# Experts' weights in pairs of chunks: 2 MB transfers with 16 KB runs, eleven slots of two chunks, and the embeddings' product kept in DRAM until the last stage

## The reference

```python
proj = x @ w_in + b_in                       # 1024 -> 5192 columns
y_attn = sparse_attention(q, k, v, indexer, rel_bias) @ w_o_attn
y_conv = silu(layer_norm(causal_conv31(a * sigmoid(g)))) @ w_o_conv
mix = (sigmoid(g_attn) * y_attn + sigmoid(g_conv) * y_conv) @ w_out
x = layer_norm(alpha * x + mix)
# mixture of experts: 32 experts, 4 for each token
for e in range(32):
    g, u = split(x @ w_gate_up[e] + b_gate_up[e])        # 1024 -> 2 x 1024
    g, u = minimum(g, 7), clip(u, -7, 7)
    y = ((u + 1) * (g * sigmoid(1.702 * g))) @ w_down[e] + b_down[e]
    out += combine[:, e:e + 1] * y                        # zero for tokens not routed to e
h = alpha * x + out
x = layer_norm(h + sigmoid(h @ w_ple_gate) * (p @ w_ple_proj))
```

## Time and profile before

| | |
|---|---|
| median of 3 runs | 1247.0 us (1243.6 to 1247.7) |
| the profiled execution's own time | 1243.07 us |
| its span in the profile | 1241.3 us |
| PE busy | 1177.9 us, 95% |
| DVE, ACT, POOL busy | 292.2, 170.7, 7.1 us |
| moved by transfers | 446.12 MB, mean 359 GB/s |
| experts' weights | 384 transfers of 1 MB |
| granted PE clock, mean | 0.984 |

### The profile page before, as it was taken

How to read it: one execution, slowest core, us unless ns; L and a number is a source line. 1 busy time by engine, 2 the same in 40 slices (tenths; PEclk the granted TensorE clock), 3 DMA queues, 4 the chain that set the end, 5 groups by cost and what they waited for, 6 DMA issues and landing times.

```text
span 1241.3 us, 14072 instructions
## 1 busy us (share of the span) xinstructions
PE 1177.9 (95%) x5694; PEld 589.4 (47%) x5694; DVE 292.2 (24%) x753; ACT 170.7 (14%) x329; POOL 7.1 (1%) x28
## 2 busy tenths in 40 slices
PE   7999999989999999998989799999999999898987
PEld 6887888853443434343334333434344333333336
DVE  0506944331121111121110211111112111111125
ACT  1213122021111101110100111111111111011012
POOL 1000000000000000000000000000000000000000
PEclk9899999999999999999989899999999999999999
DMA  9961446549999999999999999999999999999990
GB/s 314 349 195 68 146 160 261 216 171 418 421 420 422 422 421 421 420 421 422 421 421 418 414 354 398 421 421 422 421 421 419 422 422 421 421 421 421 422 354 35
DMA packets 93419, 446.12 MB, mean 359 GB/s; under 512 B 10072, under 2 KB 40064, under 8 KB 44192
## 3 DMA queue, kind: packets, MB, share of 16 engines
q1 hardware_dynamic: 89776, 440.72, 88.0%
q10 hardware_dynamic: 3200, 3.18, 0.8%
q0 software_dynamic: 368, 1.19, 0.3%
HBM read 444.00 MB, written 1.06 MB: 359 GB/s over the span
## 4 chain that ended last, share of the span: by engine, by line
PE 60%; DMA 13%; DVE 3%; ACT 1%; issue 1%; SPq 0%; DVEq 0%; ACTq 0%
PE bank L342 47%; DMA ring<-in_w_gu 9%; PE bank L330 5%; DMA arena<-in_w_gu 4%; PE bank L363 3%; PE bank L1309 2%; PE bank L349 2%; PE bank L336 1%; ACT arena L1362 1%; DVE arena L389 1%; DVE arena L383 1%; DVE arena L407 0%; DVE arena L403 0%; PE bank L1240 0%; DVE arena L399 0%
## 5 line engine op out<-in xcount | busy, mean ns | idle before, releaser
L342 PE MATMUL bank<-ring,arena 128*64 128x512 f32 x2024 | 460.4, 607 | 26.2 <-DMA ring<-in_w_gu 13.6
L342 PEld LDWEIGHTS bank<-ring,arena 128*64 128x64 f32 x2024 | 144.8, 139 | 315.4 <-issue 289.7
L342 PE MATMUL bank<-arena 128*64 128x512 f32 x1144 | 256.3, 597 | 10.3 <-DMA arena<-in_w_gu 6.8
L383 DVE TENSOR_TENSOR arena<-bank,arena 128x512 f32<-128x512 f32 x33 | 22.8, 692 | 639.2 <-PE bank L349 639.2
L342 PEld LDWEIGHTS bank<-arena 128*64 128x64 f32 x1144 | 80.5, 137 | 169.2 <-issue 158.2
L569 PE MATMUL bank<-arena,ring 128*128 128x256 f32 x576 | 130.9, 389 | 7.3 <-DMA ring<-in_w_in 7.3
L569 PEld LDWEIGHTS bank<-arena,ring 128*128 128x128 f32 x576 | 112.0, 196 | 23.9 <-issue 8.3
L1362 ACT ACTIVATE arena<-bank 128x512 f32<-128x512 f32 x62 | 37.0, 598 | 428.1 <-PE bank L342 428.1
L363 PE MATMUL bank<-arena 64*128 64x512 f32 x272 | 67.6, 615 | 1.4 <-ACT arena L1365 1.4
L330 PEld LDWEIGHTS bank<-arena 128*128 128x128 f32 x512 | 58.4, 192 | 11.4 <-issue 11.4
L330 PE MATMUL bank<-arena 128*128 128x128 f32 x512 | 61.4, 278 | 0.0
(11 more groups left out here) (196 smaller groups left out, 541.7 us busy)
## 6 DMA issues: line engine op xcount, KB each, us to landing
ring<-in_w_gu SPq DMA_DIRECT2D x160, 1024.0 KB, 26.1
arena<-in_w_gu SPq DMA_DIRECT2D x96, 1024.0 KB, 26.3
ring<-in_w_dn SPq DMA_DIRECT2D x84, 1024.0 KB, 26.3
arena<-in_w_dn SPq DMA_DIRECT2D x44, 1024.0 KB, 26.1
ring<-in_w_in SPq DMA_DIRECT2D x19, 1024.0 KB, 12.0
ring<-in_w_out SPq DMA_DIRECT2D x4, 1024.0 KB, 5.1
ring<-in_w_pg SPq DMA_DIRECT2D x4, 1024.0 KB, 19.6
ring<-in_w_oa SPq DMA_DIRECT2D x2, 1024.0 KB, 5.0
```

What stands on the lines that cost most here:

```text
L342: mm = pe.matmul(to[half * CAP:(half + 1) * CAP, :], rows, w[:, half * 512:(half + 1) * 512], start=first, stop=last)
L383: nc.vector.tensor_tensor(by_bias(gt, 8), by_bias(of_gate[:, :], 8), bias_of(e, 0, 0, 8), ALU.add).then_inc(sw_step, 1)
```

## The change

The unit of the experts' weights becomes a pair of chunks: 2 MB, 6 of them to an expert (`CPE = 6`), with 16 KB in a row in each partition: two rows of gate-and-up or four of down. There are 11 slots of a pair (22 MB where 19 MB were): 6 are the ring, 5 in the arena. A slot is freed when PE has used both halves. To match the order of rows, `gather` reads every second column of x1, `turn` every fourth column of its input, and so do the last stage's transposes of h. `w_ple_gate` is loaded as two pairs of the same form. Room is made by storing `pple` in a DRAM buffer at the end of the front stage and loading it again at the end; SP waits for that store before it issues the load of pair 10, whose slot held `pple`. The order of the first 11 loads is new; the table's transfers move from POOL to ACT, and those of b_down's rows from POOL to SP. Products and sums are the same, apart from the order of the terms.

```diff
-ES = 19
+ES = 11
 SLOT = 2048
+PAIR = 2 * SLOT
...
-CPE = 12
-DOWN_ORDER = (0, 2, 1, 3)
+CPE = 6
...
         def slot_of(n):
             i = n % ES
-            return ring[:, (NF + i) % NS, :] if i < NS else extra[i - NS]
-        def chunk_source(e, c):
-            if c < KD:
-                return w_gu[bass.ds(e, 1), c * P:(c + 1) * P, :].rearrange("e p d -> p (e d)")
-            b = DOWN_ORDER[c - KD]
-            return w_dn[bass.ds(e, 1), b * 256:(b + 1) * 256, :].rearrange("e (p r) d -> p (e r d)", r=2)
...
+            if i >= NS // 2:
+                return extra[i - NS // 2]
+            i = 2 * ((NF // 2 + i) % (NS // 2))
+            return ring[:, i:i + 2, :].rearrange("p a d -> p (a d)")
+
+        def pair_source(e, c):
+            if c < 4:
+                return w_gu[bass.ds(e, 1), c * 256:(c + 1) * 256, :].rearrange("e (p r) d -> p (e r d)", r=2)
+            return w_dn[bass.ds(e, 1), (c - 4) * 512:(c - 3) * 512, :].rearrange("e (p r) d -> p (e r d)", r=4)
...
+        x1_rows = x1.rearrange("p t (c m r) -> p t c r m", c=4, r=2)
+        h_rows = h.rearrange("p t (c m r) -> p t c r m", c=2, r=4)
...
-                    mm = pe.matmul(bank[4 + k // 4][:, (k % 4) * P:(k % 4 + 1) * P], x1[:, t, k * P:(k + 1) * P],
+                    mm = pe.matmul(bank[4 + k // 4][:, (k % 4) * P:(k % 4 + 1) * P], x1_rows[:, t, k // 2, k % 2, :],
                                    sel[:, t, :, :], start=(t == 0), stop=(t == NT - 1))
...
         def turn(pe, rows, to):
-            blocks = rows.rearrange("p (c m r) -> p c r m", c=2, r=2)
+            blocks = rows.rearrange("p (m r) -> p r m", r=4)
             for j in range(4):
-                mm = pe.transpose(to[:, j * P:(j + 1) * P], blocks[:, j // 2, j % 2, :], ident)
+                mm = pe.transpose(to[:, j * P:(j + 1) * P], blocks[:, j, :], ident)
...
+                sp.wait_ge(pple_out, 4)
+                sp.dma_start(pple_rows.rearrange("(t p) d -> p t d", p=P), pple).then_inc(pple_saved, 16)
+                sp.wait_ge(pple_saved, 16)
+                early(10)
...
+                a.wait_ge(tab_ready, 1)
+                a.dma_start(table, tab_sb[:, :]).then_inc(tab_out, 16)
...
+                a.wait_ge(tab_out, 16)
+                skew = bass.AP(tensor=table.tensor, offset=0, ap=[[1, P], [S + P, H], [1, S]])
+                a.dma_start(hankel, skew).then_inc(hankel_in, 16)
...
                 for n in range(ES, NG):
-                    sp.wait_ge(*chunk_read(n - ES))
-                    load_chunk(sp, n, n // CPE, n % CPE)
+                    sp.wait_ge(*pair_read(n - ES))
+                    load_pair(sp, n, n // CPE, n % CPE)
...
+                sp.wait_ge(*pair_read(LN2))
+                sp.dma_start(pple_t, pple_rows.rearrange("(t p) d -> p t d", p=P)).then_inc(pple_in, 16)
+                sp.dma_start(lng2, ln2g.partition_broadcast(P)).then_inc(ln_in, 16)
...
-                    for i in range(4):
-                        if i % 2 == 0:
-                            pe.wait_ge(act_ready, e * 4 + (1 + i // 2))
-                        w = weights(KD + i)
-                        for r in range(2):
+                    for i in range(2):
+                        w = weights(4 + i)
+                        for r in range(4):
+                            if i == 0 and r % 2 == 0:
+                                pe.wait_ge(act_ready, e * 4 + (1 + r // 2))
...
                     for j in range(4):
-                        if t == 0:
-                            chunk(NG + j)
                         for k in range(KD):
-                            mm = pe.matmul(gate_bank(t, j), hT[:, k, t * P:(t + 1) * P], pg_view(j)[:, k, :],
+                            if t == 0 and j == 0 and k % 4 == 0:
+                                pair(NG + k // 4)
+                            mm = pe.matmul(gate_bank(t, j), hT[:, k, t * P:(t + 1) * P], pg_view(k, j),
```

More of the change, by code:

```diff
@@ L82, in program @@
 def program(nc, x, xT, pT, w_in, bT, bki, b_in, w_oa, w_oc, w_out, dwT, convT, ln1g, ln1b, w_r, b_r,
-            w_gu, bguT, w_dn, b_dn, w_pg, w_pp, ln2g, ln2b, relb, onehot, passes, out, table):
+            w_gu, bguT, w_dn, b_dn, w_pg, w_pp, ln2g, ln2b, relb, onehot, passes, out, table, pple_rows):
     F32, I32, U32 = mybir.dt.float32, mybir.dt.int32, mybir.dt.uint32
@@ L133, in program @@
         pge = view(SC + 2048, 2048).rearrange("p (t d) -> p t d", t=NT)
-        EX = 10240
-        extra = [view(EX + SLOT * j, SLOT) for j in range(ES - NS)]
+        EX = 8192
+        extra = [view(EX + PAIR * j, PAIR) for j in (0, 1, 2, 4, 3)]
         logit = view(EX, 3072).rearrange("p (h s) -> p h s", h=H)
@@ L547, in _ @@
                 g.memset(ysb, 0.0).then_inc(zeroed, 1)
-                g.wait_ge(zeroed, 2)
-                for n in range(2):
-                    g.dma_start(ysb[n * CAP:n * CAP + NE, :], b_dn[:, n * 512:(n + 1) * 512]).then_inc(bias_rows, 16)
             @block.tensor
@@ L1136, in _, with pair @@
                 flag = pe.alloc_register("pe_two_rounds")
-                def chunk(n):
+                def pair(n):
                     pe.wait_ge(e_in[n % ES], 16 * (n // ES + 1))
@@ L1185, in use_down_twice @@
                     pe.wait_ge(act_ready, 4 * e + 4)
-                    for i in range(4):
-                        w = weights(KD + i)
+                    for i in range(2):
+                        w = weights(4 + i)
                         for a, to in ((act_b, up_turned), (act, gate_turned)):
-                            for r in range(2):
+                            for r in range(4):
                                 mm = product(pe, to, down_rows(a, i, r), w[:, r * 1024:(r + 1) * 1024],
-                                             (i, r) == (0, 0), (i, r) == (3, 1))
-                        if i < 3:
+                                             (i, r) == (0, 0), (i, r) == (1, 3))
+                        if i == 0:
                             mm.then_inc(chunk_used, 1)
@@ L1214, in one_round @@
                     q = e % 2
-                    weights = lambda c: chunk(e * CPE + c)
+                    weights = lambda c: pair(e * CPE + c)
                     turn_gates(pe, selg[:, q]).then_inc(sgt_done, 3)
@@ L1566 @@
     table = nc.dram_tensor("bias_table", (H, S + P), _mybir.dt.float32, kind="Internal").ap()
-    program(nc, *args, out, table)
+    pple_rows = nc.dram_tensor("pple_rows", (S, D), _mybir.dt.float32, kind="Internal").ap()
+    program(nc, *args, out, table, pple_rows)
     r = _run(nc, [arrays], core_ids=[0])
```

149 lines of the change are left out of this document (73 added, 76 removed).

## The result

The changed kernel takes 1235.69 us (median of 5 runs, 1235.42 to 1240.17), the kernel before 1245.84 beside it (5 runs, 1241.65 to 1247.7). The ratio is 0.9934, with a 95% interval of 0.9907 to 0.9961: faster by 0.7%. The forecast was 1226 us, a gain of 21 us on the median given then; measured are 10. The direction is right and the time lies in the range, but a little more than half of the gain is missing.

A forecast was written before the change was run, and what follows sets the result against it. Transfers bound the kernel (end 1241.3 us, PE alone about 1206); 1241.3 - 13.3 - 6 - 2.5 + 0.6 + 0.5 = 1220.6 us of span, plus 5.7 for a median of 1226, 8-in-10 range 1216 to 1285.

The forecast's parts named there:

- Longer runs: Experts' weight transfers: runs of 16 KB instead of 8 move at 427.3 GB/s, -13.3 us (0 to -27).
- Rival C: Experts' weight transfers: runs of 16 KB move no faster, span 1233.9, median 1240 us; chance 8%.
- PE in the experts: Expert stage: reading weights with a step adds 2 to 8 us, taken as +4, on PE's own end only.
- D: Experts' gathers pay in full for the column step, 70 us on PE's end, median 1283 us; chance 22%.
- B: In `turn`, step four costs 2.0 ns a column, 21 us on PE's end, median 1239 us; chance 20%.
- The front stage's +0.6: Front stage: issuing the return costs ACT about 0.6 us ahead of L818, at worst all shown on PE.
- the tie at the end: Last stage: w_ple_gate's second pair arrives about when L1309 wants it, +0.5 us (0 to 3).
- The start: Start of expert stage: ten pairs out by 262.4, pair 10 behind pple's store, -2.5 us (-5 to +4).
- The gap after two rounds: Behind the two-round expert: two more MB in flight recover lost transfer time, -6 us (0 to -7.4).
- PE's own end: End set by PE alone, without waits for weights: 1211 us, under the transfers' end, so costing nothing.

The follow-up runs named there:

- e2: e1 with each 2 MB transfer as two runs of 8 KB in a partition and the old order of rows; 1241.47 us, ratio 0.9981.
- e1: Changed kernel with SP's wait for the store of pple and pair 10's load at the head of the second block; 1230.3 us, ratio 0.9885.
- e4: Kernel before plus a store of pple and a wait for it at the end of SP's front stage; 1249.82 us, ratio 1.0049.
- f8: Changed kernel with only PE's blocks for experts of two rounds written in turned order; 1225.36 us, ratio 0.9861.
- f9: e1 with sixteen never-executed matmuls added to PE's two-round block for expert 13; 1222.68 us, ratio 0.9833.
- e5: e1 with PE's blocks for experts of two rounds written in turned order; 1223.53 us, ratio 0.9831.
- e3: Changed kernel with ten pairs of slots instead of eleven, pple kept in the arena, no store, wait or reload; 1234.05 us, ratio 0.993.
- f11: Kernel before with sixteen never-executed matmuls added to PE's two-round block for expert 13; 1243.13 us, ratio 0.9994.

## Why the prediction was half right

**Longer runs: right.** Forecast were one packet for a run and 427.3 GB/s; the rows show 24905 long packets and 427 to 428. e2 shows that this term is the runs' and not the transfers'. Measured are 421 GB/s against 427 to 428, which is 1.4% to 1.7%; the line through the two sizes of the earlier trace rows had 1.5%. Rival C is out, and that the span is 1233.9, which was C's figure too, is chance. e2 against e1 gives 9.9 us of span and 12 by the ratios, the forecast was 13.3.

**PE in the experts: right, and D false.** The gather takes 4.04 us, where L330 took 3.84 with the old order of columns, which is 0.2 a gather where I had 0.3. D's term of 70 us for 15.5 gathers is in no run; from expert to expert it is 25.32 and 28.65 (869.08, 894.40, 923.05), against 25.32 and 28.46. Step four costs as much as step two, so B is out. In the transposes a weight load takes 140 to 141 ns without a step, 209 with step two and 211 to 212 with step four (L336, L349, L357, and L1300 to L1310). The gather's loads take 192 without a step already, and a step of two adds only 4 ns. The fixed part, about 82 ns, by which I split a load into a cost for each column stands in no row, but the kernel before has loads of one column and of 32 that show it:

```profile
L759 PEld LDWEIGHTS bank<-arena x4: 79/82/83, 260.0 to 260.1; 128*1 128x1 f32 x4
L762 PEld LDWEIGHTS bank<-arena x8: 106/111/113, 260.1 to 260.3; 128*32 128x32 f32 x8
```

With L342's 64 columns in 137 ns and L330's 128 in 192 that is 82 ns and 0.86 to 0.91 ns a column. That the loads of the transposes have the same fixed part is my estimate. The front stage's +0.6 is +0.4 (SP's issue at 262.78 against 262.40, in one execution each), and the tie at the end cost nothing: L1319 runs 27.64 us without a wait.

**"The start": failed.** "Pair 10 waits for the store of pple" was priced by what the queue loses, -2.5 with +4 at worst. Pair 10 did go out at 273.77, about as worked out. What I left out is who stands behind the waiting instruction: not only pair 11, but every engine, since the block ends only when SP leaves it: in the view of L464, the block's end, the DRAIN of POOL, PE, ACT and DVE starts at 253.3 to 267.1 and SP's at 274.2, and the semaphore steps of all five come at 274.3 to 274.4. PE was 7.2 us late at the second expert (304.40 against 297.20 before). The steps e1, e4 and f8 against f9 price this at 6.1, 6.1 and 3.5 us by the ratios (4.1, 7.7 and 3.4 by the spans).

**"The gap after two rounds": failed in the kernel, right in its mechanism.** Forecast was that 2 MB of slots take 6 of 7.4 us away. It became 13.0, since the stop of 5.5 us and the slow clock keep PE from freeing slots for 7.5 us more, just where the stock is short. Without the stop and the wait 2.4 are left (e5, f9; 5.4 in f8, which has the wait), a gain of 5, and two ten-pair kernels put the eleventh pair at 5 us. Neither nor the code told of a stop that depends on the block's place; its 1.76 us stood there as a cost of the jump that I took for constant. It ended 1.43 us behind the landing of a transfer of instructions, and the changed kernel's second stop, of 5.50 us, 1.36 us behind that of the next.

**PE's own end: failed.** The 1211 us rested on the sum of PE's work and lacked both stops, 7.2 us, and 7.5 (f8 against the changed kernel) to 9.7 (e5 against e1). So PE's end came up to the transfers' end, and the 10 us of room (1220.6 against 1211) in which I had hidden the small terms were used up: PE waits only 3.6 us for weights, so its own end is near 1230. In e5, with neither stop, it waits as little and ends at 1219.1, so its own end is near 1215.5, and the sum of PE's work was short by some 4 us even there.

**The sum.** The forecast span was 1220.6. e5 and f9, with neither the wait nor the stop, have 1219.1 and 1219.2, but these were their fastest executions; by their medians, less the 1.8 us between an execution and its span, they lie at 1221 to 1222. So without the two stops the sum comes out within about 1 us. The wait at the block's end brings 2 to 3 us more (f8, 1225.36 against 1223.53 and 1222.68) and the stop 10.3 (1235.69). In the spans the stop looks like 11.3, of which some 3 are a later end of the front stage in the one profiled execution (PE enters the expert stage at 275.15 against 272.03). The forecast also put the median 5.7 above the span; the profiled execution of after was itself the median, at 1.8, so this hid 4 us of the miss. It is also by these 4 us, and so by luck, that f8, which still has the wait, lies at the 1226 us of the forecast.

What stays open: the place of the block in PE's program decides about the stop (5.73 us in e1, none in f9), and the stops end 1.35 to 1.43 us behind landings of transfers of instructions. Which instructions each 16 KB hold isn't shown, so none of these kernels could have been told beforehand to be the unlucky one. All four with the stop leave PE's blocks as the change has them, so their block stands in one and the same place; of the other places, three of the kernel before and three with pairs, none has it. That the one falls to the pairs shows nothing about pairs.

## What to carry to other kernels

A wait placed last in one engine's part of a block held all engines here (PE by 8.1, 6.0 and 8.2 us in the changed kernel, e4 and f8): put it at the head of the next block, or ahead of other work. And when two engines' ends lie as near to each other as here (1206 and 1241.3 us by the forecast's sums, 3%), a saving on one must be counted against the other's end with all its stops, not against its work alone.

## What the hardware did that was not expected

- Entering the block by a branch left PE idle for 1.7 to 2.1 us in nine kernels and for 7.1 to 7.7 us in the four others (the changed kernel, e1, e2, e3), as 1.7 to 2.0 us ahead of the first matmul and 5.4 to 5.8 us between the first and the second. Each time PE went on 1.35 to 1.43 us behind the landing of a 16 KB transfer of instructions, and two such transfers stood 5.7 to 6.2 us apart. Sixteen unexecuted matmuls ahead of the block made the difference (5.73 us between the first two matmuls in e1, none in f9).
- In the stretch 275.20:280.00, behind the wait of 8.1 us, the granted clock was 0.53, and in 664.20:675.60, behind the stop of 5.5 us, 0.50, half of full speed; the 32 matmuls of L1251 took 7.09 us there, 5.45 us in e5 (0.69 in 651.91:657.36) and L1240's 3.79 us before, in a stretch at 1.00 (662:667). Behind a short stop it was low at times: in f11, behind 1.84 us, the clock was 0.54 in 660:670, where the kernel before had 1.00 in 665.50:675.50, about as far behind its 1.76.
- In the transposes a weight load of 128 columns of float32 took 140 to 141 ns without a step, 209 ns with a step of two and 211 to 212 ns with a step of four, while the gather's loads took 192 ns without and 196 ns with a step of two.
- One queue moved 349, 421 and 427 GB/s with runs of 1, 8 and 16 KB (20:60 and 280:579.65 before, 860:960 after).
